# The sample gates' scattered store moved into the attention, and units put between the first steps of both attentions

## The reference

```python
(q, kv, gate, z_a, q_g, k_g, v_g, a_low, z_b, merge) = jnp.split(h @ w_in, _split_offsets(), axis=-1)
gate = jax.nn.sigmoid(gate.astype(F32)).reshape(B, T, 3, NSA_KV_HEADS, NSA_GROUP)
...
o_cmp, p_cmp = attend(q, kc, vc, alibi_bias(slopes, dist_c), (dist_c >= 0)[None, None])   # compressed keys
...
o_nsa = gate[:, :, 0, :, :, None] * o_cmp + gate[:, :, 1, :, :, None] * o_slc + gate[:, :, 2, :, :, None] * o_win
mix = jax.nn.sigmoid(g_a) * (o_nsa @ w_ba) + jax.nn.sigmoid(g_b) * (o_g @ w_bb)
return x + mix @ w_out
```

## Time and profile before

| | |
|---|---|
| median of 3 runs | 1389.58 us (1387.01 to 1389.69) |
| profiled execution: its own time | 1381.97 us |
| its span | 1380.1 us |
| PE busy | 1307.4 us, 95% |
| DVE, ACT, POOL busy | 46%, 45%, 11% |

### The profile page before, as it was taken

One profiled execution on the slowest core, in us unless ns is written; L12 is line 12 of the kernel. 1 busy time (PEld: TensorE's weight loads), 2 busy tenths in 40 slices (PEclk: granted clock), 3 DMA queues, 4 the chain that ended last, 5 costly groups with the idle time before them and its releaser, 6 DMA issues.

```text
span 1380.1 us, 23623 instructions
## 1 busy us (share of the span) xinstructions
PE 1307.4 (95%) x9533; PEld 1174.8 (85%) x9533; DVE 632.7 (46%) x1395; ACT 623.8 (45%) x1072; POOL 151.9 (11%) x185
## 2 busy tenths in 40 slices
PE   5999998998999999999999999999988988999998
PEld 5999998998978888988988889788865678999876
DVE  6211145644834343433233332467588766453342
ACT  6212236542465546555456545665476542221121
POOL 2100001103300000100000300313010270000000
PEclk9999999999999999999999999999998999999999
DMA  7251453422321211222212212545254746542231
GB/s 203 65 169 35 140 122 103 144 67 55 83 63 52 69 47 58 63 75 67 63 57 78 63 57 68 177 150 149 87 192 149 238 152 191 159 134 84 96 126 61
DMA packets 156908, 145.27 MB, mean 105 GB/s; under 512 B 27360, under 2 KB 141360, under 8 KB 156736
## 3 DMA queue, kind: packets, MB, share of 16 engines
q1 hardware_dynamic: 154016, 135.33, 32.5%
q0 software_dynamic: 2784, 8.43, 2.1%
HBM read 105.88 MB, written 41.88 MB: 107 GB/s over the span
## 4 chain that ended last, share of the span: by engine, by line
PE 65%; DVE 5%; ACT 2%; issue 2%; POOL 1%; DMA 0%; POOLq 0%; DVEq 0%; another core or an unknown queue 0%; SPq 0%; ACTq 0%
PE ps L240 38%; PE ps L2545 6%; PE ps L1671 5%; PE ps L1705 4%; PE ps L1687 4%; PE ps L1720 1%; POOL oL L2594 1%; DVE S L2656 1%; PE ps L1790 1%; PE ps L2553 1%; PE ps L1641 0%; PE ps L2512 0%; PE ps L1744 0%; PE ps L1624 0%; ACT sP L2262 0%
## 5 line engine op out<-in xcount | busy, mean ns | idle before, releaser
L240 PE MATMUL ps<-hH,wH 128*128 128x352 f32 (+1 forms) x1320 | 441.0, 334 | 11.5 <-ACT stg L360 6.0
L240 PE MATMUL ps<-hH,wL 128*128 128x352 f32 (+1 forms) x1320 | 426.1, 323 | 0.0
L240 PE MATMUL ps<-hL,wH 128*128 128x352 f32 (+1 forms) x1320 | 425.8, 323 | 0.0
L240 PEld LDWEIGHTS ps<-hH,wH 128*128 128x128 f32 (+1 forms) x1320 | 248.9, 189 | 38.5 <-issue 26.9
L240 PEld LDWEIGHTS ps<-hL,wH 128*128 128x128 f32 (+1 forms) x1320 | 249.9, 189 | 2.2 <-issue 1.9
L240 PEld LDWEIGHTS ps<-hH,wL 128*128 128x128 f32 (+1 forms) x1320 | 248.7, 188 | 0.3
L227 DVE TENSOR_TENSOR wL<-w_raw,wH 128x1024 fp32r<-128x1024 f32 (+1 forms) x70 | 85.7, 1225 | 135.3 <-ACT wH L219 135.2
L2023 DVE CUSTOM_DVE_ANT_0 sP<-ps,dist,stat 128x256 f32<-128x256 f32 (+3 forms) x116 | 58.5, 542 | 181.8 <-issue 104.4
L360 ACT ACTIVATE stg<-ps 128x352 f32<-128x352 f32 x132 | 61.0, 462 | 116.4 <-PE ps L240 107.6
L219 ACT ACTIVATE wH<-w_raw 128x1024 fp32r<-128x1024 f32 (+1 forms) x70 | 73.5, 1049 | 70.8 <-issue 39.5
L2219 ACT ACTIVATE pPT<-ps 128x512 f32<-128x512 f32 x74 | 44.0, 595 | 134.7 <-PE ps L1687 134.7
(11 more groups left out here) (395 smaller groups left out, 2069.8 us busy)
## 6 DMA issues: line engine op xcount, KB each, us to landing
w_raw<-in_w_in SPq DMA_DIRECT2D x61, 512.0 KB, 4.1
p_spill<-stg SPq DMA_DIRECT2D x132, 176.0 KB, 1.8
zt<-p_spill SPq DMA_DIRECT2D x24, 528.0 KB, 4.8
w_raw<-in_w_in SPq DMA_DIRECT2D x17, 256.0 KB, 3.8
gvT<-p_spill SPq DMA_DIRECT2D x8, 528.0 KB, 5.6
x_all<-in_x_prompt SPq DMA_DIRECT2D x8, 512.0 KB, 9.2
m_raw<-in_w_branch_b SPq DMA_DIRECT2D x8, 512.0 KB, 5.4
xr<-in_x_prompt SPq DMA_DIRECT2D x8, 512.0 KB, 3.5
```

The lines of the kernel that those rows point to most:

```text
L240: mm = nc.tensor.matmul(ps[0:t.m, bank, 0:NF], w[:, c % 2, t.m * k:t.m * k + t.m], x[n][:, k, :], start=(k == 0 and i == 0), stop=(k == t. ...
```

## The change

Three things are edited.

1. `store_gates`, eight transfers of 96 numbers of 4 bytes each, goes from the first block's SP to the third block's, behind the stores of units 27 and 28. The load of grow goes from the second block to the second round (r == 1) of the third block's loop, and DVE waits for it in the first `output`.
2. In the compressed attention, ACT's first two exponentials stand between the copies of units 27, 28 and 29 and no longer ahead of them.
3. Two units, 39 and 40, are computed between `scores(0)`, `scores(1)` and `scores(2)`, with their DVE part behind `score(1)` and `score(2)` and their ACT part ahead of the first exponentials of the main loop. The cuts up to 49 share two units fewer: 76 and not 78.

```diff
-            def store_gates():
-                sp.wait_ge(sem("gate_ready"), 2)
-                for b in range(DB):
-                    sp.dma_start(gate_spill[b].rearrange("x t c -> t c x"),
-                                 gate[DS * b:DS * b + DS, PT, :].rearrange("t (c x) -> t c x", c=3),
-                                 allow_slow_non_contiguous=True).then_inc(sem("gate_spilled"), 16)
...
             store_tokens()
-            store_gates()
+            sp.wait_ge(sem("gate_ready"), 2)
             sp_units(sp, 9)
...
-            sp.wait_ge(sem("gate_spilled"), 16 * DB)
-            sp.dma_start(grow, gate_spill.rearrange("(q b) x t c -> (b x t) q c", q=2)).then_inc(sem("grow_loaded"), 16)
             sp_units(sp, 6)
             sp.wait_ge(sem("hid_done"), 2)
             load_w1(sp, 1)
             sp_units(sp, 12)
-            sp.wait_ge(sem("grow_loaded"), 16)
...
-        UA = NE - 39
+        AHEAD = 39 + 2
+        UA = NE - AHEAD
...
             for m in range(LA):
+                if m >= 1:
+                    pe_units(pe)
                 scores(m)
...
                 gcol = (1, 2, 0)[br]
+                if u == 0:
+                    dve.wait_ge(sem("grow_loaded"), 16)
...
             dve_units(dve)
             for m in range(LA):
                 score(m)
+                if m >= 1:
+                    dve_units(dve)
...
+            act_units(act)
             cmp_exp(0)
+            act_units(act)
             cmp_exp(1)
-            act_units(act, 3)
+            act_units(act)
...
             copy(aupS[:, :], aupR[:, :]).then_inc(sem("aup_high"), 1)
+            act_units(act, 2)
...
+            sp_units(sp, 2)
+            for b in range(DB):
+                sp.dma_start(gate_spill[b].rearrange("x t c -> t c x"),
+                             gate[DS * b:DS * b + DS, PT, :].rearrange("t (c x) -> t c x", c=3),
+                             allow_slow_non_contiguous=True).then_inc(sem("gate_spilled"), 16)
             for r in range(R - 1):
-                sp_units(sp, 39 + UA * min(M0, last_cut(16 * r + 15) + 5) // M0 - unit["sp"])
+                if r == 1:
+                    sp.wait_ge(sem("gate_spilled"), 16 * DB)
+                    sp.dma_start(grow, gate_spill.rearrange("(q b) x t c -> (b x t) q c", q=2))\
+                        .then_inc(sem("grow_loaded"), 16)
+                sp_units(sp, AHEAD + UA * min(M0, last_cut(16 * r + 15) + 5) // M0 - unit["sp"])
```

More of the change, by code:

```diff
@@ L1554, in hybrid_step @@
                        "qk_loaded", "raw_read", "elem_done", "v_loaded0", "v_loaded1", "kp_loaded2", "kp_loaded3", "kp_loaded4",
-                       "kp_loaded5", "at_done", "w4_done", "tails_ready", "qi_ready", "k4_copied"]
+                       "kp_loaded5", "at_done", "w4_done", "tails_ready", "qi_ready", "k4_copied", "grow_loaded"]
         for name in decode_sems:
```

## The result

The changed kernel takes 1375.61 us (median of 6 runs, 1371.63 to 1382.71), the kernel before 1386.84 us (6 runs, 1383.36 to 1389.69). The ratio is 0.9922, with a 95% interval of 0.9906 to 0.9937: 11 us, or 0.8%, faster. The forecast was 7.5 us faster and 1382.1 us; the sign was right, the time lies 3.0 us under the range's low end. Of the 6.5 us between forecast and measurement 2.7 are the kernel before itself, whose median of six runs is that much under that of the first three; 3.7 us are gain that the sum lacked.

What follows compares the result with a forecast made beforehand. TensorE, busy 1307.4 of 1380.1 us, was taken to bound the kernel, so only its standstills and slow clock could be won. 4.1 + 0 + 3.4 = 7.5 us off the median 1389.58 gave 1382.1 us; range 1378.6 to 1386.2.

Steps and rivals of the forecast that it cites:

- Stall 1: PE's pause at 190 us behind the gates' store: 2.5 us of pause and 1.6 of clock, 4.1 us won.
- The gates at the new place: Gates' transfers behind the stores of units 27 and 28, and grow's load: cost 0, hidden by at least 2.4 us.
- Stall 2: PE's 3.67 us wait before unit 29, near 332 us: two shorter waits replace it; between +0.9 and -0.7, taken as 0.
- Stall 3: PE's pauses between the first scores, 392 to 398 us: units cover them, 3.4 us won, no clock loss counted.
- The main loop: Long stretch, 655 to 860 us without PE idle: 76 units for 78, time only moves, nothing won or lost.
- the gating wait: PE's 2.7 us wait for DVE's gating of a unit, at m = 9: it stays.
- The sum: Whole kernel: 4.1 + 0 + 3.4 = 7.5 us won, giving 1382.1 us from the median 1389.58; forecast's chance 0.64.

Runs made afterwards that it cites:

- parts_1_3: The changed kernel with both first exponentials back ahead of the three copies; ratio 0.9945 to the kernel before, 7.6 us won.

## Why the prediction named the right pauses and was too small

The pauses went and came as forecast; what failed is the price of each. 1375.6 us lies outside the stated range because two of the three terms were too small, and it would lie further off if the third had not been too large.

- **Stall 1** (4.1 us). The pause went, by the means forecast. The term was too large: 2.5 us of pause and 1.6 us of clock were forecast, and 1.8 us measured alone (0.1 to 3.3) and 1.7 beside the other parts. The clock's fall is mostly not saved but moves: six of the seven profiles with the pause at 190 us have the fall there and none at 215, the seventh has it at 215; of the eleven without the pause, seven have it at 215.
- **The gates at the new place** (0). Right: issue from 341 to 347, landing behind it 10.4 to 11.2 us, no wait of PE, and none with twice as many. Nothing shows a cost of the load of grow.
- **Stall 2** (0). The two waits that take the old one's place are as forecast, 2.5 and 1.6 us for 2.7 and 1.7, and unit 30 starts 6.9 us behind cmp_exp(1) where it was 7.8: 0.9 us. The choice of 0 between +0.9 and -0.7 was too low: in eight of the nine profiles with part 2 and three units the clock did not fall there. Alone the part measured 0.6 us, beside the other two 2.8, more than the forecast's best case. Part of that is that the old pause cost more than was read from one profile: 3.3 us of clock, and not 1.8, in three of the seven profiles that have it. The rest is not shown.
- **Stall 3** (3.4 us). This is the step that failed, together with the 0 for stall 2. "The two shorter pauses of stall 3 did not [lose the clock]" was read from a single execution. In the six other profiles with these pauses the clock fell, five times for 3.3 us and once for 1.8. The term put this clock at nothing, and measured 5.4 us alone and 5.7 us beside the others.
- **The main loop** (0). Right: PE is as busy as before (a wait of 0.4 us came between 420 and 450 us, and one of 0.4 us between 510 and 540 went), and the gating wait stays at 2.6 us.
- **The sum.** 1.7 + 2.8 + 5.7 = 10.2, against 10.4 measured as the mean of four. Against 4.1 + 0 + 3.4 that is 2.4 less, 2.8 more and 2.3 more; that the sum is off by 3 us and not 5 is luck. The mistake behind the terms is that one execution stood for all. The first profile was one with a high clock (0.987; 68 others of the kernel before average 0.9834, and four of them reach 0.987), 5 us faster than their median, and the stretches at 390 and 480 us have no loss in it where the other two profiles lose 5.1. Adding its distance from the median as a constant hid this: part of that distance is what the change removes. Another 2.7 us of the miss are the kernel before itself, whose median of six runs is lower than that of the first three.

What stays open: why three parts are worth 10.4 us together and 7.8 one by one. The table suggests that a fall depends on the pauses before it (the fall at 480 is rare only where both earlier pauses are gone or filled), but each cell is one execution, and no run moved a pause alone. And whether the gates' move is worth its 1.7 us beside the other parts is open too: the two pairs measured on one chip each say 0.2 and 3.6 us, and each of their ratios is known to some 3 us.

## What to carry to other kernels

In this kernel a pause of PE of 2 to 4 us costs its length and often a fall of the clock, 1.8 us or two of these. Filling it can be worth more than its length (3.4 us of pauses gave 5.4 to 5.7) or less, where the fall only moves to the next pause (2.4 us gave 1.8). Compare a profile's own time and mean clock with those of the other runs before a sum is made from it: the falls that it happens not to show are in the median. To compare two profiles, take the start of one instruction behind the last edit in both: here the first two profiles differ there by 4.6 us, while their spans differ by 0.5 us the wrong way. When a scattered store stalls what is queued behind it, either put it where there is cover or write it in rows and scatter the reading; both gave the same here.

## What was not expected of the hardware

- The clock's falls are not the same from one execution of a kernel to the next: at the same two pauses at 392 us the kernel before lost 0, 3.3 and 3.3 us in its three profiles. The Trainium skill (TensorE: Matmul & The Clock Gate, Part 1) says that how many matmuls run at the lower level varies from run to run of one kernel, by what the chip's clock control is doing at the kernel's start. These profiles show the variation in the middle of a kernel.
- A fall avoided at 190 us often comes at 215, behind a pause of 2.1 us at which, after a fall at 190, there was none in six of six profiles.
- The slow stretch behind scattered writes did not grow from 8 transfers to 16: the load behind 16 landed in 10.3 to 11.2 us. Behind 8 at the same place it was 8.0 to 11.9 us in the changed kernel's four profiles, and 14.7 at the most in parts_1_3.
